# Two half projections between four modulation blocks at the start of the first mixer

## The reference

```
mod = silu(c) @ w_ada + b_ada                 # c: 1 x 1024, w_ada: 1024 x 6144
shift1, scale1, gate1, shift2, scale2, gate2 = split(mod, 6)
h    = rms_norm(x, norm1_g) * (1 + scale1) + shift1
proj = h @ w_in                               # 256 x 1024 @ 1024 x 5120
q_sb, k_sb, v_sb, q_mb, k_mb, v_mb, g_sb, g_mb = split(proj, ...)
```

## Time and profile before

| | us |
|---|---|
| median of 3 runs | 1561.27 (1561.07 to 1564.43) |
| the profiled execution, its own time | 1563.33 |
| span of the profiled execution | 1561.5 |
| PE busy in it | 1330.1 (85%) |
| DVE busy | 545.3 (35%) |
| ACT busy | 406.3 (26%) |
| share of the hardware DMA queue that carries the weights | 83.8% |
| mean granted TensorE clock | 0.926 |

### The profile page before, as it was taken

One profiled execution on the slowest core, in us unless ns is written; L12 is line 12 of the kernel. 1 busy time (PEld: TensorE's weight loads), 2 busy tenths in 40 slices (PEclk: granted clock), 3 DMA queues, 4 the chain that ended last, 5 costly groups with the idle time before them and its releaser, 6 DMA issues.

```text
span 1561.5 us, 24381 instructions
## 1 busy us (share of the span) xinstructions
PE 1330.1 (85%) x10184; PEld 903.2 (58%) x10184; DVE 545.3 (35%) x1197; ACT 406.3 (26%) x624; POOL 0.2 (0%) x4
## 2 busy tenths in 40 slices
PE   6989999899999999989699999999777557657656
PEld 2878997566666565556388999999323113113112
DVE  2526765434323232321375675754301001001001
ACT  3437753111111110101164346453201000000001
POOL 0000000000000000000000000000000000000000
PEclk7999999999999999999999999999888788788778
DMA  9886449799999999999943644546999999999996
GB/s 364 273 298 246 167 164 401 283 394 380 421 421 415 421 416 420 416 410 421 402 164 108 216 162 145 180 164 270 411 422 418 421 422 418 422 422 419 422 422 248
DMA packets 118745, 523.53 MB, mean 335 GB/s; under 512 B 10968, under 2 KB 15480, under 8 KB 71032
## 3 DMA queue, kind: packets, MB, share of 16 engines
q1 hardware_dynamic: 115664, 519.69, 83.8%
q10 hardware_dynamic: 2984, 2.44, 0.5%
HBM read 520.85 MB, written 1.24 MB: 334 GB/s over the span
## 4 chain that ended last, share of the span: by engine, by line
PE 59%; DMA 18%; SPq 16%; DVE 3%; ACT 2%; issue 2%; DVEq 0%; ACTq 0%
PE psum L1952 17%; PE psum L2399 9%; SPq L646 8%; PE psum L2454 5%; SPq L653 5%; DMA ring<-in_w_up_e_dram 5%; DMA ring<-in_w_exp_up_dram 3%; PE psum L2335 3%; DMA ring<-in_w_exp_down_dram 3%; PE psum L2324 2%; SPq L657 2%; DMA ring<-in_w_down_e_dram 2%; DMA ring<-in_w_in_dram 2%; PE psum L2846 2%; DMA arena<-in_w_exp_down_dram 2%
## 5 line engine op out<-in xcount | busy, mean ns | idle before, releaser
L1952 PE MATMUL psum<-arena_r,ring_r 128*128 128x256 f32 x2400 | 290.8, 282 | 6.0 <-DVE arena_r L1124 3.1
L1952 PEld LDWEIGHTS psum<-arena_r,ring_r 128*128 128x128 f32 x2400 | 284.9, 189 | 11.9 <-issue 6.1
L2399 PE MATMUL psum<-ring,arena 128*32 128x256 f32 (+1 forms) x2304 | 185.1, 393 | 14.1 <-DMA ring<-in_w_up_e_dram 13.3
L1117 DVE TENSOR_TENSOR ring_r<-ring,ring_r 128x1024 fp32r<-128x1024 f32 x140 | 163.1, 1220 | 89.2 <-ACT ring_r L742 88.4
L2399 PEld LDWEIGHTS psum<-ring,arena 128*32 128x32 f32 (+1 forms) x2304 | 111.6, 124 | 79.8 <-issue 23.9
L2846 PE MATMUL psum<-ring,arena 128*32 128x512 f32 x720 | 111.4, 749 | 49.0 <-DMA ring<-in_w_exp_up_dram 43.0
L742 ACT ACTIVATE ring_r<-ring 128x1024 fp32r<-128x1024 f32 x140 | 137.5, 1050 | 49.9 <-DMA ring<-in_w_in_dram 35.2
L2863 PE MATMUL psum<-ring,arena 128*32 128x512 f32 x384 | 76.7, 837 | 66.9 <-DMA ring<-in_w_exp_down_dram 48.4
L2454 PE MATMUL psum<-ring,arena 128*32 128x512 f32 (+1 forms) x576 | 95.4, 622 | 6.0 <-DMA ring<-in_w_down_e_dram 5.0
L2846 PEld LDWEIGHTS psum<-ring,arena 128*32 128x32 f32 x720 | 22.4, 124 | 115.5 <-DMA ring<-in_w_exp_up_dram 64.2
L2863 PEld LDWEIGHTS psum<-ring,arena 128*32 128x32 f32 x384 | 18.8, 142 | 118.8 <-issue 88.9
(11 more groups left out here) (408 smaller groups left out, 1452.6 us busy)
## 6 DMA issues: line engine op xcount, KB each, us to landing
ring<-in_w_gate_e_dram SPq DMA_DIRECT2D x64, 1024.0 KB, 14.4
ring<-in_w_up_e_dram SPq DMA_DIRECT2D x64, 1024.0 KB, 14.6
ring<-in_w_down_e_dram SPq DMA_DIRECT2D x64, 1024.0 KB, 14.6
ring<-in_w_exp_gate_dram SPq DMA_DIRECT2D x45, 1024.0 KB, 26.1
ring<-in_w_exp_up_dram SPq DMA_DIRECT2D x45, 1024.0 KB, 26.0
ring<-in_w_exp_down_dram SPq DMA_DIRECT2D x40, 1024.0 KB, 26.7
ring<-in_w_in_dram SPq DMA_DIRECT2D x19, 2048.0 KB, 9.1
ring<-in_w_ada_dram SPq DMA_DIRECT2D x12, 2048.0 KB, 13.7
```

What stands on the lines that cost most here:

```text
L1117: V.tensor_tensor(lo, whole, hi.bitcast(F32), ALU.subtract).then_inc(w_low, 1)
L1952: ins = product(lambda a_, b_, k, first, last: mm(ps[:, t * T:(t + 1) * T], a_[:, k, c], b_[:, k, :], start=first, stop=last), w, x, None ...
L2399: ins = mm(psum[c, 5, 256 * g:256 * g + 256], xg1[:, k, P * j + width * b:P * j + width * (b + 1)], weight(g, e, k), start=(k == 0), stop= ...
```

## The change

Chunks in0 and in1 are both loaded and multiplied by halves of k. SP now loads ada0 and ada1, the upper halves of in0 and in1 (1 MB each), ada2 and ada3, then the lower halves of in0 and in1, and goes on with in2. ada2 and ada3 no longer go through the ring: they land in `buf(11)` with `buf(12)` and in `buf(4)` with `buf(5)`, which are free at this time, with semaphores of their own (`load_away`). All later ring slots move by two; the memory columns, which land in `buf(11)`, wait for ada2's product. PE multiplies ada0, ada1, the upper half of in0, ada2, half of the upper half of in1, ada3, `columns(2)`, a quarter, `columns(3)`, the last quarter, and then the lower halves of in0 and in1. The slots of in0 are given back by the first matmul of in1's lower half. ACT and DVE split the upper quarters of both chunks after the first half of `h`, and the lower quarters after the second half; the split of in2 follows at c = 0, that of in3 at c = 1, none at c = 2, and from c = 3 on it is as before.

```diff
+ADA_RING = 2
+CHUNKS_A = [("w_ada", 512 * ADA_ORDER[_j], 512, 8) for _j in range(ADA_RING)]
...
+SPLIT_BEHIND = {0: 2, 1: 3, 3: 4, 4: 5, 5: 6}
+def split_count(k, q):
+    return 4 * (q // 2) + 2 * k + q % 2 + 1 if k < 2 else 4 * k + q + 1
...
+        ada_away = [buf(11, SLOT), buf(4, SLOT)]
...
+            for n in range(ADA_RING):
+                load(ring[:, SLOT_A[n], :], CHUNKS_A[n], load_a[SLOT_A[n]])
+            for c in range(2):
+                input_half(c, 0, first_in[c])
+            for n in range(2):
+                load(ada_away[n], ("w_ada", 512 * ADA_ORDER[ADA_RING + n], 512, 8), load_away[n])
+            for c in range(2):
+                input_half(c, 1, None)
...
             rms_act(1, rstd_of(1))
-            for n in range(3):
+            for n in range(2):
                 ada_copy(n)
             act.wait_ge(normed, 1)
             x_high_part("h1", 0)
+            high(0, (0, 1))
+            high(1, (0, 1))
+            ada_copy(2)
             ada_copy(3)
-            high(0, (0, 1))
             act.wait_ge(normed, 2)
             x_high_part("h1", 1)
             high(0, (2, 3))
+            high(1, (2, 3))
             for c in range(6):
-                high(1 + c)
+                if c in SPLIT_BEHIND:
+                    high(SPLIT_BEHIND[c])
...
+            for n in range(ADA_RING):
                 modulation(n, n)
-            columns(ADA_FIRST - 1).then_inc(mod_full, 1)
+                columns(n).then_inc(mod_full, 1)
+            input_products(0, 0, 0)
+            input_products(0, 0, 1)
+            modulation(2, None)
+            input_products(1, 0, 0)
+            modulation(3, None)
+            pe.wait_ge(mod_ready, 1)
+            columns(2).then_inc(mod_full, 1)
+            input_products(1, 0, 1, range(1))
+            columns(3).then_inc(mod_full, 1)
+            input_products(1, 0, 1, range(1, 2))
+            for c in range(2):
+                for j in range(2):
+                    input_products(c, 1, j, gives=(used_a, 2) if c and not j else None)
+            held = (used_a, 2)
+            for c in range(2, 6):
```

More of the change, by code:

```diff
@@ L147 @@
 IN_A = {}
-CHUNKS_A = [("w_ada", 512 * ADA_ORDER[_j], 512, 8) for _j in range(ADA_FIRST)]
+ADA_RING = 2
+CHUNKS_A = [("w_ada", 512 * ADA_ORDER[_j], 512, 8) for _j in range(ADA_RING)]
 for _c in range(10):
@@ L180 @@
 SPLIT_AT = {x: k for k, x in enumerate(SPLIT)}
+SPLIT_BEHIND = {0: 2, 1: 3, 3: 4, 4: 5, 5: 6}
+def split_count(k, q):
+    return 4 * (q // 2) + 2 * k + q % 2 + 1 if k < 2 else 4 * k + q + 1
 JOBS = ["rel"]
-JOBS += ["ms1", "sum1"] + [f"ada{_j}" for _j in range(ADA_FIRST)]
-for _c in range(6):
+JOBS += ["ms1", "sum1", "ada0", "ada1", "in0_0", "in0_1", "ada2", "in1_0", "ada3", "in1_1"]
+for _c in range(2, 6):
     JOBS += [f"in{_c}_{_j}" for _j in range(2)] + {3: ["ms0"], 4: ["sum0"]}.get(_c, []) + [f"ada{_j}" for _j in ADA_BEHIND.get(_c, ())]
@@ L409, in build @@
         load_x = [sem(f"added_slot{i}_loaded") for i in range(RING2 - RING)]
-        first_in = sem("first_input_half_loaded")
+        first_in = [sem(f"first_input_half_loaded{i}") for i in range(2)]
+        load_away = [sem(f"modulation_block_loaded{i}") for i in range(2)]
         load_ahead = sem("block_ahead_loaded")
@@ L535, in load @@
                     sp.dma_start(dst, a["w_gate_sh"][0].rearrange("(k p) f -> p k f", p=P)).then_inc(done, 16)
[L536 to L540, removed]
                 else:
@@ L556, in _, with input_half @@
             sp.dma_start(xT, a["x_columns"].rearrange("p (k t) -> p k t", t=T)).then_inc(x_in, 16)
+            def input_half(c, h, landed):
+                s = SLOT_A[IN_A[c]] % RING
+                dst = ring[:, s, :].rearrange("p (k c) -> p k c", k=KT)
+                sp.dma_start(dst[:, 4 * h:4 * h + 4, :],
+                             a["w_in"][0, 512 * h:512 * h + 512, 512 * c:512 * c + 512].rearrange("(k p) c -> p k c", p=P))\
+                  .then_inc(load_a[s] if landed is None else landed, 16)
+            for n in range(ADA_RING):
[6 more added lines that the diff above has]
+                input_half(c, 1, None)
             for n, spec in enumerate(CHUNKS_A):
+                if n <= IN_A[1]:
+                    continue
                 if SLOT_A[n] >= RING:
@@ L564, in _ @@
                 if n == IN_A[3]:
+                    full(sp, "ada2")
                     sp.dma_start(memN, a["mem_columns"].rearrange("p (k t) -> p k t", t=T)).then_inc(mem_in, 16)
@@ L727, in high @@
                 for q in quarters:
-                    if k == 0 and q == 0:
-                        act.wait_ge(first_in, 16)
-                    if q == (2 if k == 0 else 0):
+                    if k < 2 and q == 0:
+                        act.wait_ge(first_in[k], 16)
+                    if q == (2 if k < 2 else 0):
                         arrived(act, SPLIT[k])
@@ L1114, in low_part @@
                 for q in quarters:
-                    dve.wait_ge(w_high, 4 * k + q + 1)
+                    dve.wait_ge(w_high, split_count(k, q))
                     whole, lo, hi = split_views(k, q)
@@ L1188, in _ @@
                 x_low_part("h1", half)
-                low_part(0, (0, 1) if half == 0 else (2, 3))
+                for k in range(2):
+                    low_part(k, (0, 1) if half == 0 else (2, 3))
             for c in range(6):
@@ L1195, in _ @@
                     ins.then_inc(mem_normed, 1)
-                low_part(1 + c)
+                if c in SPLIT_BEHIND:
+                    low_part(SPLIT_BEHIND[c])
                 if c == 2:
@@ L2036, in modulation @@
             def modulation(n, place, gives=None):
-                w = chunk_a(place, 512)
+                if ADA_RING <= n < ADA_FIRST:
+                    pe.wait_ge(load_away[n - ADA_RING], 16)
+                    w = ada_away[n - ADA_RING].rearrange("p (k c) -> p k c", k=KT)
+                else:
+                    w = chunk_a(place, 512)
                 if n == 0:
@@ L2050, in modulation @@
                     columns(n - 1, gives=(used_a, 1)).then_inc(mod_full, 1)
-                elif n != ADA - 2:
+                elif n != ADA - 2 and not ADA_RING <= n < ADA_FIRST:
                     full(pe, f"ada{n}")
@@ L2068, in _ @@
             norm_total(1, part_x)
[L2069 to L2073, removed]
-                modulation(n, n)
-            columns(ADA_FIRST - 1).then_inc(mod_full, 1)
[L2077 to L2096, removed]
@@ L2098, in _, with input_products @@
-            held = None
-            for c in range(6):
+            n0 = IN_A[9] - 9
+            def input_products(c, half, j, ts=range(2), gives=None):
+                hi, lo = PARTS["h1"]
+                w = chunk("a", IN_A[c], whole=False)
+                name = f"in{c}_{j}"
+                ps = bank(name) if half or ts[0] else start(name)
+                for t in ts:
+                    cols = slice((2 * j + t) * P, (2 * j + t + 1) * P)
+                    for k in range(4 * half, 4 * half + 4):
+                        if j == 0 and t == 0 and k % 2 == 0:
+                            pe.wait_ge(x_low, 4 * PART_AT["h1"] + k // 2 + 1)
+                            pe.wait_ge(w_low, split_count(c, k // 2))
+                        for i, (a_, b_) in enumerate(((w[0], hi), (w[0], lo), (w[1], hi))):
+                            ins = mm(ps[:, t * T:(t + 1) * T], a_[:, k, cols], b_[:, k, :], start=(t == 0 and k == 0 and i == 0),
+                                     stop=(k == KT - 1 and i == 2), skip_group_check=True)
+                            if gives is not None and t == 0 and k == 4 * half and i == 0:
+                                ins.then_inc(*gives)
+                if half and ts[-1] == 1:
+                    done(ins, name)
@@ L2100, in _ @@
+            for c in range(2):
[3 more added lines that the diff above has]
+            for c in range(2, 6):
                 w = chunk("a", IN_A[c], whole=False)
-                if c == 0:
-                    project_by_halves(w)
                 for j in range(2):
@@ L2107, in _ @@
                         project_rows(f"in{c}_{j}", w, ("h1", 0), j, arriving, gives)
-                    elif c:
+                    else:
                         project(f"in{c}_{j}", w, ("h1", 0), 2 * j, arriving, gives)
```

## The result

The changed kernel takes 1574.72 us (median of 6 runs, 1573.63 to 1577.70), the kernel before beside it 1564.15 (6 runs). The ratio is 1.0072, 95% interval 1.0059 to 1.0086, so the change costs between 9 and 13 us. The forecast was 10.8 us more, 1572.1.

A forecast was written before the change was run, and what follows sets the result against it. Bounds at the head: in1's end on PE and in4's landing, set by the release of in0's slots. Release at 47.4 + 5.3 + 5.7 + 2.3 = 60.7, 10.8 late; 1561.27 + 10.8 = 1572.1 us, range 1566.4 to 1576.

The forecast's parts named there:

- First halves: Head of the kernel: upper halves arrive early, so PE starts in0 at 29.9 instead of 37.15.
- The loss at the low clock: From PE's start of in0 at 29.9: 1.6 us lost at 1.2 GHz, bounds 0 and 3.35.
- `columns(3)`: End of PE's first-half list: at 47.4 instead of 35.9, so the second half of `h` comes 11.5 us later.
- The wait through DVE and ACT: Between `columns(3)` and PE's lower halves: a 5.3 us chain, in which PE idles 3.9 us.
- Clock behind the pause: Second halves of in0 and in1: the clock falls again after 3.9 us idle, costing 2.3 us, between 0 and 3.35.
- 0.50 after idle: Rows at 20.0 and 95.1, cited as the clock at half rate after idle, in support of the 2.3 us loss.
- Release and stream: in0's slots given back at 60.7, 10.8 us late; stream unchanged, so in4 lands 40.7 us later, at 101.4.
- What is late next: `columns(5)`, behind in4's split, at 106.9; added idle time covers PE's own 5.1 us, so 10.8 is passed on.
- only PE's delay: Rival: stream up to in4 has slack, so in1's end on PE decides; +5.1 us, 1566.4; chance 0.10.
- The rest moves as it is: Behind in4: later loads are issued against slots PE gives back, so everything moves along with the 10.8 us.
- The sum: Whole kernel: +10.8 us on the median of 1561.27 makes 1572.1; likeliest case 1568 to 1575.
- Worse: Rival: clock low over second halves and longer at in4, another 3.35 on top of 13.5, up to 1578; chance 0.06.

The follow-up runs named there:

- e3: The changed kernel, with in1's upper half multiplied behind ada3 and both `columns` instead of between them; 1568.21 us against 1562.88 for the kernel before, ratio 1.0038.
- e6: The changed kernel, with nine matmuls of constants put into PE's 3.8 us pause ahead of the lower halves; ratio to the kernel before 1.0060.
- e8: The kernel before, with twelve matmuls of constants (5.2 us on PE) behind ada4 and ahead of in3; 3.5 us more, ratio 1.0025.
- e1: The kernel before, with in0's slots given back by the first matmul of in1's second bank instead of its first; 1568.75 us against 1562.88, ratio 1.0035.
- e2: The changed kernel, with the memory columns and eight bias reads issued right behind in2; 3.7 us above the kernel before, ratio 1.0023.
- e7: The kernel before, with twelve matmuls of constants (5.2 us on PE) between in1 and in2; 4.1 us more, ratio 1.0025.
- e4: The kernel before, with the memory columns and eight bias reads issued behind in2 instead of in3; 1560.37 us against 1562.88, ratio 0.9986.
- e5: The changed kernel with the edits of both e2 and e3; 1560.64 us against 1562.49 for the kernel before, ratio 0.9990.

## Why the prediction was right

The mechanism came out as forecast: the second half of `h` is late, the ring slots of in0 come back late, and the load stream behind them brings in4 late by as much. Where the numbers agree more closely than the steps do, it is said.

**First halves.** 29.9 forecast, 29.60 measured. The loss at the low clock was taken as 1.6; 48 records took 7.17, at 0.118 each they are 5.7, so 1.5.

**`columns(3)`** at 47.4 forecast, 46.8 measured, 10.9 later than before (11.5 forecast). in2 starts 4.2 us later than before (65.35 against 61.12), where 5.1 was forecast for PE.

**The wait through DVE and ACT** was 5.3; from 46.76 to PE's start at 52.11 it is 5.35, of which PE stood 3.84 (3.9 forecast). e3 shows its cause: with the whole upper half of in1 as cover it disappears.

**Clock behind the pause.** 2.3 was taken, the term that was mis-sized: 1.4 by e6. The Trainium skill, "TensorE: Matmul & The Clock Gate", Part 1, says that half rate is the default and that activity releases it; the trace agrees in direction (0.50 from 53.1 to 56.4 behind a pause, 1.00 in e6 where the pause was filled). But of the two rows that the prediction gave for "0.50 after idle" only the one at 95.1 is of that kind. In the other the clock was still at 1.00 up to 19.5 and fell at 20.0, while PE multiplied ada1, and the longest pause of PE in the 7 us before was 0.88 us.

**Release and stream.** Release 10.8 late forecast, 9.8 measured (`columns(3)` was early and the clock cost less). The stream was taken as unchanged. From SP's issue it was 40.4 before and 41.5 after. The two errors, 1.0 each, cancel at in4: 101.4 forecast, 101.49 measured, and that they do is luck. The 1.05 goes with the rate of the bias reads in the one profiled execution of each kernel. In the 7 us from 15.8 us behind SP's issue the DMA engines moved 186 GB/s in e8, 176 in e6, 167 before, 155 in e3, 145 in e1 and 144 in the changed kernel, and the streams took 39.4, 40.3, 40.4, 40.6, 41.2 and 41.5 us, in the same order. Why the rate differs was not tested. That this stream passes the release on is shown by e1 (release alone, 5.9 us), e3 (in1 early on PE, and still 5.3 us) and e2 (a stream shorter by 10, in4 earlier by 10).

**What is late next.** Forecast was that PE's own 5 us are covered and do not add. In the changed kernel they do not (106.89 against 106.9). ada6 waited 1.95 us for its load at 96.09, which was not forecast and costs nothing at `columns(5)`, since PE would have waited for in4 behind it. The prediction's own numbers had it: ada6 lands one 2 MB transfer, 5.4 us, ahead of in4, so at about 96.0, and PE was to come to it at 95.1. But the reason given, that the pause absorbs PE's delay, holds only because the stream was late by more: e7 and e8 show that with the stream on time 5.2 us of PE cost 3.5 to 4.1. So the 5.1 us of the rival "only PE's delay" would have been nearly the right cost if the release had stayed on time; with the late release the stream decided.

**The rest moves as it is.** The shift is 10.8 us at `columns(5)` and at the start of in4, as forecast, and 11.75 at the attention. The sum had nothing for the low clock in in4 itself, 0.80 more than before; the prediction has it only in its rival "Worse". The whole kernel shows 11.3 by the ratio and 10.6 by the medians, so it can't tell 10.8 from 11.75. Over the kernels of the table the shift at the attention and the time go together within 1.3 us but for e7 (2.0 against 4.1, interval 2.3 to 5.6). e7's profiled execution was a short one: its span is only 2.3 us above that of the kernel before (1563.8 against 1561.5), so the 2.0 fits that execution, and the rest is a difference between executions.

## What to carry to other kernels

Before work is moved into a gap of an engine, list what its later instructions give back: here the half products filled 7 us of idle PE time and delayed the return of two ring slots by 10, and the loads behind them were the path. A pause of an engine ahead of a landing is slack only if no load further on waits for what that engine does after the delay; follow each gate (here four: in0's end, in2's start, ada4's start, and ada5 with the `columns` behind it) to its landing. Loads that need no ring slot belong in the stretch where the DMA engines stand still, not in the queue behind a release; in the kernel before, moving them (e4) brought 2.5 us, with an interval of 0.5 to 3.7.

## What the runs showed of the hardware

While the eight bias reads of 128 KB were in flight, the DMA engines moved 167 GB/s in the kernel before (a window from 66 to 73) and 160 in e4 (47 to 56), and were full all the same (share 1.14 and 1.13), while the weight loads go at 387. Placed in a gap they are as slow: in e4 the slow stretch is 9 us long and reaches past the release at 50.50 into the stream behind it.

In the changed kernel the clock fell at 53.0, when PE had been working again for 0.9 us after the pause of 3.84 us, and not during it. In the kernel before it fell at 95.0, in the pause. It also fell behind shorter waits: at 97.5, behind one of 1.95 us.

What a pause costs by the low clock was not the same from case to case, nor did the longer pause cost more: 1.4 us behind 3.84 us (e6), 1.6 behind 3.39 (e4's in5, 12.85 against 11.21 at full clock), 2.6 behind 4.10 (in4 before), and 3.2 behind 3.11 (e5's `columns` and in5, 1.86 and 13.57 against 1.05 and 11.21).
